# Value and gate columns of a hybrid decoder layer projected in a Strassen sweep of their own, between the two passes

## The reference

```python
u = rms_norm(h, norm_gain) * (1.0 + scale) + shift
proj = u @ w_in        # 1024 x (512 pool v | 512 pool gate | 512 r | 512 k | 512 v | 64 wd | 64 ad | 512 rwkv gate)
y_pool = multiscale_pool(proj[pool v]) * silu(proj[pool gate])
p = proj[r|k|v|wd|ad]; p = p + (token_shift(p) - p) * mu
w_log = -softplus(-(w0 + tanh(wd) @ w_lora_up)) - 0.5;  decay = exp(-exp(w_log))
a = sigmoid(a0 + ad @ a_lora_up);  kk = normalized(k * k_k);  k = k * (1 + (a - 1) * k_a)
# per head of 64: S_t = S_{t-1} diag(w_t) + (S_{t-1} a_t) b_t^T + v_t k_t^T ;  y_t = S_t r_t
y = group_norm(wkv7_scan(r, decay, k, v, -kk, kk * a)) + sum(r * k * r_k) * v
y_rwkv = y * silu(proj[rwkv gate])
h = h + gate * (concat(y_pool, y_rwkv) @ w_out);  return rms_norm(h, final_gain)
```

## Time and profile before

| | us |
|---|---|
| median of 3 runs | 2581.05 (2577.9 to 2581.61) |
| the profiled execution | 2582.14 |
| its span, first to last instruction | 2580.4 |
| TensorE busy in the span | 2489.7 |
| VectorE busy | 1657.4 |
| ScalarE busy | 1147.4 |
| end of the last project product of the first pass | 656.9 |
| Gram matrices of block 0 of the second pass | 753.4 |

### The profile page before, as it was taken

One profiled execution on the slowest core, in us unless ns is written; L12 is line 12 of the kernel. 1 busy time (PEld: TensorE's weight loads), 2 busy tenths in 40 slices (PEclk: granted clock), 3 DMA queues, 4 the chain that ended last, 5 costly groups with the idle time before them and its releaser, 6 DMA issues.

```text
span 2580.4 us, 73686 instructions
## 1 busy us (share of the span) xinstructions
PE 2489.7 (96%) x30485; PEld 2054.8 (80%) x30485; DVE 1657.4 (64%) x3459; ACT 1147.4 (44%) x2539; POOL 415.3 (16%) x565
## 2 busy tenths in 40 slices
PE   4999999999999999999999999999999999999995
PEld 4777666777768888888888888888888888888883
DVE  4563344334357777777777777767777777777774
ACT  4332223331124555454455554544555445455552
POOL 1410111110111111111111111211111112111110
PEclk7999999999999999999999999999999999999997
DMA  6613321334510010000001010000110000001000
GB/s 236 208 63 130 130 98 56 114 122 172 187 50 10 35 35 33 28 26 26 26 26 43 26 35 26 26 26 26 35 35 28 33 26 26 26 26 43 26 19 25
DMA packets 72618, 152.91 MB, mean 59 GB/s; under 512 B 3801, under 2 KB 38190, under 8 KB 71342
## 3 DMA queue, kind: packets, MB, share of 16 engines
q1 hardware_dynamic: 68878, 141.62, 15.6%
q10 hardware_dynamic: 3488, 7.34, 0.8%
HBM read 98.61 MB, written 50.33 MB: 58 GB/s over the span
## 4 chain that ended last, share of the span: by engine, by line
PE 85%; DVE 9%; issue 3%; ACT 1%; DMA 1%; SPq 0%; DVEq 0%; ACTq 0%
PE banks L1183 21%; PE banks L383 15%; PE banks L1164 14%; PE banks L1218 9%; PE banks L459 9%; PE banks L1238 7%; DVE SM L1830 2%; PE banks L1281 1%; PE banks L1294 1%; PE banks L1194 1%; PE banks L1348 1%; PE banks L1270 1%; DMA gc<-in_w_ada 1%; PE banks L1302 1%; PE banks L1303 1%
## 5 line engine op out<-in xcount | busy, mean ns | idle before, releaser
L1183 PE MATMUL banks<-xT,wts 128*128 128x128 f32 x5232 | 633.7, 279 | 0.0
L1183 PEld LDWEIGHTS banks<-xT,wts 128*128 128x128 f32 x5232 | 598.2, 192 | 30.9 <-issue 27.1
L1493 ACT ACTIVATE LX<-banks 128x512 f32<-128x512 f32 (+1 forms) x384 | 185.0, 524 | 643.4 <-DVE WT L1774 437.3
L1164 PE MATMUL banks<-xT,wts 128*64 128x128 f32 x6944 | 420.1, 274 | 0.0
L1164 PEld LDWEIGHTS banks<-xT,wts 128*64 128x64 f32 x6944 | 380.2, 137 | 6.3
L1610 POOL TENSOR_TENSOR BK<-k,egi 64x512 f32<-64x512 f32 x64 | 96.0, 1500 | 930.4 <-ACT egi L1462 889.4
L1218 PE MATMUL banks<-wo,Y 128*128 128x512 f32 x512 | 233.8, 600 | 4.7 <-DVE Y L1734 4.7
L383 PE MATMUL banks<-ts,wts 128*128 128x256 f32 x1024 | 233.3, 381 | 0.0
L1774 DVE TENSOR_TENSOR WT<-banks,level_mask 128x256 f32<-128x256 f32 x256 | 102.6, 422 | 194.8 <-PE banks L1238 186.8
L459 PE MATMUL banks<-wo,yc 128*128 128x512 f32 x512 | 224.1, 596 | 0.0
L383 PEld LDWEIGHTS banks<-ts,wts 128*128 128x128 f32 x1024 | 195.9, 191 | 27.5 <-DVE fgain L845 0.5
(11 more groups left out here) (193 smaller groups left out, 3649.1 us busy)
## 6 DMA issues: line engine op xcount, KB each, us to landing
wo<-in_x SPq DMA_DIRECT2D x8, 2048.0 KB, 9.4
xt_dram<-xT SPq DMA_DIRECT2D x32, 512.0 KB, 8.6
xr<-in_x SPq DMA_DIRECT2D x32, 512.0 KB, 5.7
h_dram<-xr SPq DMA_DIRECT2D x32, 512.0 KB, 2.7
xT<-xt_dram SPq DMA_DIRECT2D x32, 512.0 KB, 3.3
gate_row<-h_dram SPq DMA_DIRECT2D x32, 512.0 KB, 3.4
out<-gate_row SPq DMA_DIRECT2D x32, 512.0 KB, 2.6
wts<-in_w_in SPq DMA_DIRECT2D x4, 2048.0 KB, 7.9
```

The lines of the kernel that those rows point to most:

```text
L1164: last = nc.tensor.matmul(o[half(c)], lhsT[:, half(c)], rhs, start=start, stop=stop)
L1183: last = (by_halves if halves else nc.tensor.matmul)(bank[b][:, q * P:(q + 1) * P], w2_tile(k, t0 + q), xT[par][:, k, :], start=(k == 0), ...
L1493: s(nc.scalar.activation(to, of, ACT.Copy), lx_ready, hold=False)
```

## The change

**A sweep of its own.** The four value and four gate tiles are no longer projected in the second pass's blocks. After the last output unit of the first pass, eight rounds (`NS`) of 512 tokens load `xT` back from `xt_dram`, and project value and gate columns in pairs with the 7 products of the first pass (`sweep_pair`). ScalarE and VectorE make silu of the gate and the token shift of the value there (`value_prev`, `value_shift`). Both results are stored to `v_dram` and `g_dram` by block of 128 tokens, and the second pass loads them a block at a time (`vm`, `rgate`). The weights of the sweep are loaded into the first pass's place and their sums made anew (`sweep_weights`).

**The second pass** keeps 9 tiles in three groups: low rank, keys, receptance; 18 slots with fewer in each `fill`. The last group is taken from PSUM after `state_and_output(1)`. VectorE's `shift(n+1, 2)` now stands ahead of `new_key`. Its value shift, gate clamp, gate product, `decay_ahead`, two of three tanh operations and the four scalings of `new_key` are gone or moved; ScalarE makes the latter in `key_factor`, and tanh by Ln and Exp in `sigmoid_tanh`.

**Start and seam.** The sums of the first pass's weights move from VectorE to POOL, the gate's modulation sum and `out_weights` move later into block 1, and the prologue of the second pass stands behind the sweep, with no output units behind it.

```diff
-            GROUPS = [(12, 1, 0), (0, 4, 1), (4, 4, 0), (8, 4, 1), (13, 4, 0)]
-            MIXED = [1, 5, 9, 13]
+            GROUPS = [(LORA_AT, 1, 0), (4, 4, 1), (0, 4, 0)]
+            MIXED = [1, 5, 9]
...
                 for i in range(2 * J1):
                     out_unit(N1 - 2, i)
-                meanwhile()
                 for i in range(2 * J1):
                     out_unit(N1 - 1, i, ahead=False)
+                for m in range(NS):
+                    for g in range(NP):
+                        sweep_pair(m, g)
+                meanwhile()
...
+                for m in range(NS):
+                    for g in range(NP):
+                        take_p1(N1 + m, g)
...
+                        gate_exp(N1 + m, g, gs[m % 2], gcs)
...
+                        value_prev(m, g)
...
                 sp.wait_ge(xT_stored, 16 * J1 * N1)
-                first_loads()
-                load_w2(3)
...
+                load_xs(0)
+                load_xs(1)
                 store(N1 - 2)
                 swap_residual(N1 - 1)
                 store(N1 - 1)
+                for m in range(1, NS):
+                    sp.wait_ge(mm_ps.sem, mm_ps.at(N1 + m - 1, 7 * PT))
+                    if m + 1 < NS:
+                        load_xs(m + 1)
+                    else:
+                        load_w2(0)
+                        first_loads()
+                    store_vg(m - 1)
...
                     for i in range(STEPS - 1):
                         step(i)
-                        fill(3 if i < LV else 2)
                         if i in (2, 3):
                             other(i - 2)
+                        else:
+                            fill(2)
...
                     solve(0)
                     fill(2, halves=True)
                     state_and_output(0, first)
-                    fill(2, halves=True)
+                    fill(1, halves=True)
                     if ahead:
                         key_norm()
                     from_state(1)
+                    solve(1)
                     fill(1, halves=True)
-                    solve(1)
-                    fill(2, halves=True)
                     state_and_output(1)
                     fill(len(SLOTS), halves=True)
...
                     take_r(1)
                     if ahead:
-                        decay_ahead()
+                        shift(n + 1, 2)
                         new_key()
                     state_sum(1)
                     if ahead:
                         taken_key()
-                        shift(n + 1, 3)
                         decayed_key()
...
-                pool.wait_ge(xT_stored, 16 * J1 * N1)
-                pool.wait_ge(yc_ready1.sem, yc_ready1.at(N1 - 1, 2))
...
+                pool.wait_ge(mm_ps1.sem, mm_ps1.at(N1 + NS - 1, 7 * PT))
+                pool.wait_ge(vg_stored, 32 * J1 * NS)
+                nc.gpsimd.memset(prev[:, :, 0:1], 0.0).then_inc(zero_ready, 1)
```

More of the change, by code:

```diff
@@ L497, in tensor @@
                 project(0, first=True)
-                pe.wait_ge(gate_used, KT)
                 s.block(0)
[L500 to L504, removed]
+                s.wait(sum_ready, 7 * (PT - 1) + C22)
                 for k in range(KT):
                     transpose_unit(1, k, BANK_T[k % 4])
-                project(1, late=(wo1_ok, 1))
+                for g in range(PT):
+                    if g == PT - 1:
+                        gate_total()
+                    project_pair(1, g, second=True)
+                pe.wait_ge(wo1_ok, 2)
                 between(1, first=True)
@@ L840, in combine @@
                         s.wait(p1_ready, g + 1)
-                    elif step == C11 and g == 0:
+                    elif step == C11 and g == 0 and low is None:
                         s.wait(halo_ready, 1)
@@ L891, in residual, with pairs @@
                     nc.vector.tensor_tensor(xr[:, j, o], bank[BANK_OUT[h]][:, :], xr[:, j, o], ALU.add).then_inc(h_ready.sem, 1)
-                def pairs(n, first=False):
+                def pairs(n, first=False, second=False):
                     for g in range(PT):
+                        if second and g == PT - 1:
+                            out_weights()
                         combine(n, g, U2)
@@ new lines, in sweep_sum, with value_shift @@
+                def sweep_sum(m, i):
+                    right_sum(N1 + m, i, xs[m % 2], tss[m % 2], (xs_in[m % 2], 16 * J1 * (m // 2 + 1)))
+                def value_shift(m, g):
+                    s.block(m)
+                    s.wait(vin_ready, g + 1)
+                    nc.vector.scalar_tensor_tensor(out=vs[m % 2][:, g, :], in0=vs[m % 2][:, g, :], scalar=omu[:, 8 + g:9 + g],
+                                                   in1=vprev[:, g, 0:T1], op0=ALU.mult, op1=ALU.add).then_inc(v_ready1.sem, 1)
@@ L1139, in run @@
                         load_xT(n + 2, par)
+                    if ahead:
+                        sp.wait_ge(vt_ps.sem, vt_ps.at(n, 1))
+                        sp.wait_ge(prep_ready.sem, prep_ready.at(n, 1))
+                        load_values(n + 1)
+                    if not first:
+                        sp.wait_ge(y2_ready.sem, y2_ready.at(n - 1, 1))
+                        load_gate(n)
                     if not first:
@@ L1431, in take_group, with sigmoid_tanh, key_factor @@
                         t = t0 + q
-                        nx(nc.scalar.activation(prev[:, t, 1:], src, ACT.Copy, scale=v("mu", t)), mix_in, hold=False)
+                        nx(nc.scalar.activation(prev[:, t, 1:], src, ACT.Copy, scale=v("mu", MU_AT[t])), mix_in, hold=False)
                 def exp_tanh():
                     hd.wait(mix_ready, 1)
-                    hd(nc.scalar.activation(th[0:LORA, :], mix[0:LORA, 12, :], ACT.Exp, scale=-2.0), eth_ready)
+                    hd(nc.scalar.activation(th[0:LORA, :], mix[0:LORA, LORA_AT, :], ACT.Exp, scale=-2.0), eth_ready)
+                def sigmoid_tanh():
+                    hd.wait(tclamp_ready, 1)
+                    hd(nc.scalar.activation(th[0:LORA, :], th[0:LORA, :], ACT.Ln, bias=1.0), t_own)
+                    hd(nc.scalar.activation(th[0:LORA, :], th[0:LORA, :], ACT.Exp, scale=-1.0), ts_ready)
+                def key_factor():
+                    hd.wait(sig_ready, 2)
+                    for p in range(NP):
+                        hd(nc.scalar.activation(t2[:, p], sig[:, 1, p], ACT.Identity, scale=v("k_a", p), bias=oka[:, p:p + 1]),
+                           kmul_ready, hold=False)
                 def exp_low_rank(i):
@@ L1532, in run @@
                     take_step(1)
-                    if not first:
-                        pv.wait(y2_ready, 1)
-                    s(nc.scalar.activation(rgate[:, :, :], rg[:, :, :], ACT.Exp, scale=-1.0), erg_ready)
+                    if ahead:
+                        sigmoid_tanh()
                     take_step(2)
@@ L1578, in scalar @@
                 exp_tanh()
-                for gr in range(1, 5):
-                    take_group(0, gr)
+                sigmoid_tanh()
+                take_group(0, 1)
                 exp_low_rank(0)
```

461 lines of the change are left out of this document (297 added, 164 removed).

## The result

The changed kernel takes 3031.56 us (median of 4 runs, 3030.39 to 3032.08), the kernel before 2580.55 beside it (4 runs): ratio 1.175, 95% interval 1.1736 to 1.1764. The prediction was 3020, range 2875 to 3085. Between the two profiled spans lie 3028.6 - 2580.4 = 448.2 us.

What follows compares the result with a forecast made beforehand. TensorE's work was taken as the bound, only just covering other engines' chains at two places. 2580.4 - 8 (start) + 387 (sweep) + 19 (seam) + 41 (blocks) = 3019, given as 3020 us; range 2875 to 3085.

Steps and rivals of the forecast that it cites:

- The slots covered chains: Second pass's blocks: of 15 us taken from TensorE only 3.2 are seen, 53.8 us a block at full clock.
- The end of the block: Last state piece to Gram matrices: the chain through ScalarE and VectorE takes 11.8 us, where it was 8.5.
- ScalarE's wait: Middle of the block: TensorE waits 3.3 us for ScalarE ahead of state_and_output(1), 12.8 us after from_state(0).
- The clock: Block's end: TensorE's wait lowers its clock in every block, costing 4.5 us a block, bounds 0 and 7.
- the 0.8 that the prediction gave as a sign: Second pass: granted clock near 0.8; the prediction is wrong if the clock stays at 1.0.
- Sweep: After the first pass: 8 rounds of 4 pairs at 12.09 us each add 387 us, TensorE full.
- Seam: Between the passes, around the sweep: 61 us ahead and 54 behind, 115 against 96.5, so +19, bounds +8 and +45.
- Start: First pass's start: weight sums moved to POOL shorten TensorE's wait for the modulation sum, -8 us, bounds 0 and -20.
- Rival 2: Blocks: both chains overlap with state work, a block takes 42 us, the kernel 2512; decided from 44.1 downwards; 4%.
- Rival 1: Blocks: the clock stays up, a block takes 53.8 us and the kernel 2880; 22%.
- rival 3: Middle of the block: clock down there too, 3 us a block more, 61.5 and above, the kernel 3115; 10%.

Runs made afterwards that it cites:

- Run 8: The kernel before, with the blocks' value and gate tiles projected by one of their eight matmuls each, all else unchanged and no sweep: 2577.82 us, ratio 0.9992.
- Run 1: The changed kernel with eight matmuls more per block, results unread, in pairs in TensorE's four longest waits: 2969.96 us, ratio 1.1513.
- run 2: The changed kernel with VectorE's k, state sum, kk, t and BK ahead of the block's last shift, rk behind it: 2869.73 us, ratio 1.1128.
- run 3: The changed kernel with the last slot moved from behind state_and_output(1) to ahead of it: 2952.97 us, ratio 1.1448.
- run 6: Run 5's kernel with GpSimd's two BK pieces waiting until VectorE's BK is done: 2825.13 us, ratio 1.0947.
- run 9: The changed kernel with the orders of run 2 and run 3, GpSimd's BK pieces last, taken_key ahead of state_sum(1), ScalarE's order kept: 2804.86 us, ratio 1.0866.
- Run 5: The changed kernel with the orders of run 2 and run 3, and ScalarE's take_u(1) ahead of key_factor and key_scale: 2869.69 us, ratio 1.1123.
- Run 4: The changed kernel with the first pass's four weight sums back on VectorE, nothing else: 3023.07 us, ratio 1.1719.
- run 7: Run 5's kernel with two matmuls, results unread, in TensorE's wait ahead of variance: 2871.7 us, ratio 1.1122.
- run 10: Run 9's kernel with four matmuls more a block, results unread, ahead of the second state piece, variance and the Gram products: 2805.41 us, ratio 1.0868.

## Why the prediction was right

**The slots covered chains.** This was the step that carried the forecast. Run 8 shows it for the part from the state work to the Gram products. The prediction also had the two parts apart: by its terms 27.8 us for the first (34.9 - 8 x 0.97 + 0.7) and 12.8 + 1.4 + 11.8 = 26.0 for the second, 53.8 at full clock. Run 1, at full clock, has 28.9 and 27.2, 56.03 in all: a miss of 2.2 us, half of it in each part. That the second part grew, from 22.1 us, is the change's own order and not only cover lost: runs 2, 3 and 6, put together in run 9, took it back by order, to 22.0.

**The end of the block: mis-sized by one operation.** 11.8 us predicted from the state piece's end to the Gram products, 12.9 measured. `t` was taken at 0.73 us, as a plain operation; it took 1.65, as before, since its form was not what made it slow (run 6: 0.69). The Trainium skill has the rule ("SBUF — State Buffer", "SBUF: two separate sides"): a VectorE operation with two SBUF inputs and a GpSimd operation that reads SBUF exclude one another at a shared pair of ports, for a whole instruction. The traces agree: `t` ends 0.55 us after GpSimd's last piece in the changed kernel (2027.64 against 2027.09) and in the kernel before (1539.32 against 1538.77). `stmp`, which reads `banks`, was not slowed beside a piece: it was taken at 0.9 and took 0.88.

**ScalarE's wait.** 3.3 us predicted ahead of `state_and_output(1)`, 2.32 measured, although `key_factor` took 1.65 us for the 1.14 taken. The stretch from `from_state(0)` to this point came out as predicted, 2016.56 - 2003.53 = 13.0 us for 12.8. Run 5 took the wait away and gained nothing over run 2: the wait came back ahead of variance.

**The clock.** 4.5 us a block predicted; the rows show 3.3 (run 1), and 2.0 is what a full clock was worth. The windows of the block shown have not one low stretch but several: 0.57 at 2016 to 2020 us, then 0.87, 0.50, 0.93, and 0.50 again under the Gram products. The waits, too, are four of 2.1 to 2.3 us, where the prediction had most of the waiting in one stretch. Over the second pass the clock is 0.88, for the 0.8 that the prediction gave as a sign. The low clock does come back in every block (the Gram products took 3.8 us in each of 28), as the Trainium skill's page that the prediction names has it. The clock term was too large by 2.5 us and the chain too small by 2.2; they cancelled, and the block came out at 58.0 for 58.3. The mechanism stands, but the closeness of the block is luck.

**Sweep.** 387 predicted, 386.9 measured, as 32 pairs of the first pass's own rows.

**Seam.** +19 predicted, +26.7 measured: 67.4 us ahead of the sweep for 61, with waits of 3.05 us for `yc` and 5.31 for the residual (6 predicted for both), and 59.0 us of output units for 55.3, at clock 0.92; 55.8 behind it for 54, with the wait for the stores of `g_dram` 7.29 as part of it.

**Start.** This step failed: -8 predicted from moving the weight sums to POOL, -0.2 measured. Run 4 shows why: with the sums on VectorE the start is 7.3 us shorter. In the changed kernel the modulation sum stands at 59.8 us for 49.46, so the move lost time instead of gaining it; what the rest of the new first pass gained, about as much, made up for it. That the two sum to -0.2 is chance.

**Rival 2** (chains fold, faster below 44.1 us a block) was the only one with another sign. The best order reached 50.81, so about 7 us a block would still have to go. Rival 1's block of 53.8 with the clock up and the changed order was not reached (56.03).

**Sums of the prediction that do not close.** For rival 2 it says that 8.6 us of VectorE's work stand behind the last slot; its own terms give 9.4 with the shift, 8.3 without. For rival 3 two state pieces and two slots are 4.6 us of work by its rows, not 3. And the upper end of the range takes a block of 60.3 us, where its own bounds (56 at full clock, 7 for the clock) reach 63. The forecast of 3020 uses none of the three.

## What to carry to other kernels

An engine that is 96% busy need not be the bound everywhere: where its work fills waits of other chains of the same length, taking it away gives nothing, and one run that only leaves the work out, before the change is built, tells so (run 8: 12.8 us a block less work, 0.1% less time). Leave it out where the change would, and read the result part by part: here one part of the block could give 6 us and the other nothing. Price the chain of the other engines first, with the order in which they stand: one reordering of VectorE was worth 162 us, the pace that came back with it included, and filled waits alone 62. Work moved to GpSimd is not free for VectorE where both read SBUF.

## What was not expected of the hardware

Two-input operations of VectorE and GpSimd side by side hold one another up: 128x2048 takes 2.35 us alone and 6.41 beside GpSimd's, 128x512 takes 0.69 and 1.65; `stmp`, with one input in PSUM, takes 0.88 beside GpSimd's piece and away from it (run 6). Adding 7.9 us of matmuls a block made the kernel 62 us faster, by holding the granted clock at 1.00. And the clock's gain does not add to that of the order: filling all four waits was worth 62 us in run 1, and on the reordered chain filling one (run 7) or three (run 10, where the clock was at 0.98 already) was worth nothing.
